# Latent attention with the keys on the partitions, in place of queries on the partitions and transposed probabilities

## What is computed

```python
def mla_attend(qn, qr, kn, kr, v):
    s = (jnp.einsum('bqhd,bkhd->bhqk', qn, kn, preferred_element_type=jnp.float32)
         + jnp.einsum('bqhr,bkr->bhqk', qr, kr, preferred_element_type=jnp.float32)) * MLA_SCALE
    p = jax.nn.softmax(s, axis=-1)
    o = jnp.einsum('bhqk,bkhd->bqhd', p.astype(v.dtype), v)
    return o.reshape(qn.shape[0], qn.shape[1], H_B * V_B)
```

## Time and profile before

| | us |
|---|---|
| median of 3 runs | 3316.15 |
| lowest and highest of the runs | 3316.11, 3319.95 |
| span of the profiled execution | 3312.2 |
| the stage, first product to the first of `mix_and_route` | 305.3 |
| TensorE busy in the span | 3117.9 (94%) |
| VectorE, ScalarE, GpSimd busy in the span | 1331.6, 780.3, 621.2 |

### The profile page before, as it was taken

The page is one execution under the profiler, slowest core; times in us unless marked ns, Lnnn a source line. Parts: engine busy times, 40 slices in busy tenths (PEclk is TensorE's granted clock), DMA queues, the critical chain, the costliest instruction groups (busy, mean ns, idle before and its releaser), DMA issues. The chain is left out here.

```text
span 3312.2 us, 35441 instructions
## 1 busy us (share of the span) xinstructions
PE 3117.9 (94%) x14154; PEld 1647.6 (50%) x14154; DVE 1331.6 (40%) x2223; ACT 780.3 (24%) x1548; POOL 621.2 (19%) x519
## 2 busy tenths in 40 slices
PE   7998989999949999599999988999999999999998
PEld 3457656665424444244456656444444444444443
DVE  2226437673351111524322465314525444544233
ACT  3126534442211111312212036111011211111001
POOL 0005400000000110023022125322203232321323
PEclk9999999999969999699999999999999999999999
DMA  7210000003267885501000130012101111113443
GB/s 287 76 51 29 1 26 1 1 1 155 115 249 295 331 332 174 202 32 38 29 24 27 52 134 2 32 51 95 70 38 51 51 39 39 50 38 141 137 132 130
DMA packets 65826, 311.38 MB, mean 94 GB/s; under 512 B 10240, under 2 KB 11776, under 8 KB 51840
## 3 DMA queue, kind: packets, MB, share of 16 engines
q1 hardware_dynamic: 61056, 292.35, 23.6%
q0 software_dynamic: 4608, 16.78, 2.0%
HBM read 272.39 MB, written 36.70 MB: 93 GB/s over the span
## 5 line engine op out<-in xcount | busy, mean ns | idle before, releaser
L2697 PE MATMUL banks<-hT,ffn_ring 128*128 128x512 f32 x528 | 235.7, 596 | 1.1 <-PEq L2393 1.1
L2857 PE MATMUL banks<-down_ring,down_sums 128*128 128x512 f32 x440 | 189.2, 592 | 0.0
L2697 PEld LDWEIGHTS banks<-hT,ffn_ring 128*128 128x128 f32 x528 | 101.0, 192 | 128.4 <-issue 128.3
L822 PE MATMUL banks<-kT_b,qT_b 96*128 96x512 f32 (+1 forms) x384 | 158.7, 523 | 3.5 <-ACT prob_b L884 2.4
L2697 PE MATMUL banks<-ffn_row_sums,ffn_w_sums 128*128 128x512 f32 x352 | 158.3, 592 | 1.2 <-DVE ffn_row_sums L2737 1.2
L330 PE MATMUL banks<-w_in,hT 128*128 128x512 f32 (+1 forms) x384 | 157.5, 567 | 1.2 <-PEq L157 1.2
L2747 DVE SCALAR_TENSOR_TENSOR ffn_acc<-ffn_u,s_ffn_taps,ffn_acc 128x1023 f32<-128x1023 f32 x88 | 125.0, 1421 | 68.0 <-ACT ffn_acc L2730 66.4
L2857 PEld LDWEIGHTS banks<-down_ring,down_sums 128*128 128x128 f32 x440 | 83.6, 190 | 105.2 <-issue 103.8
L728 POOL TENSOR_TENSOR prob<-prob,softmax_columns 128x640 f32<-128x640 f32 (+1 forms) x64 | 75.4, 1199 | 312.4 <-DVE softmax_columns L686 312.4
L1592 PE MATMUL banks<-hT,side_ring 128*128 128x512 f32 x256 | 127.5, 617 | 1.3 <-PEq L2208 1.3
L2666 POOL TENSOR_TENSOR ffn_w_sums<-ffn_ring 128x512 f32<-128x512 f32 x22 | 35.1, 1596 | 473.8 <-DMA ffn_ring<-in_w_ffn 344.2
(11 more groups left out here) (509 smaller groups left out, 5379.4 us busy)
## 6 DMA issues: line engine op xcount, KB each, us to landing
down_ring<-in_w_down SPq DMA_DIRECT2D x132, 256.0 KB, 2.9
expert_wg<-in_w_gate SPq DMA_DIRECT2D x16, 2048.0 KB, 15.4
expert_wu<-in_w_up SPq DMA_DIRECT2D x16, 2048.0 KB, 20.8
expert_wd<-in_w_down SPq DMA_DIRECT2D x16, 2048.0 KB, 8.5
ffn_ring<-in_w_ffn SPq DMA_DIRECT2D x22, 1024.0 KB, 4.8
wmod_slab<-in_w_mod SPq DMA_DIRECT2D x6, 2048.0 KB, 7.9
wmod_ring<-in_w_mod SPq DMA_DIRECT2D x4, 2048.0 KB, 10.9
w_out<-in_w_out SPq DMA_DIRECT2D x4, 2048.0 KB, 8.5
```

The costliest lines, as they stand in the source:

```text
L822: last = nc.tensor.matmul(scores(u)[:, a:b], heads[u // 2].q[u % 2], heads[u // 2].keys[u % 2][:, a:b], start=True, stop=True, skip_group_ ...
L2697: last = nc.tensor.matmul(product(f, m), wt[:, q, :], x[:, q, :], start=q == 0 and m != 2, stop=q == 3, skip_group_check=True)
L2857: last = nc.tensor.matmul(c.bank(4 - 4 * (p % 2) + t), stationary[:, P * t:P * t + P], w[s % RING][:, 0, :], start=j == 0, stop=j == N - 1)
```

## The change

`attend_by_keys` takes the place of `attend_latent`. Its unit `u` is a pair of heads and 256 queries; there are 16. The scores are made the other way round, with 128 keys on the partitions and 2 x 256 queries along the row: ten key tiles `j` of 128 x 512, one PSUM bank each, four banks in turn. Probabilities then have the keys on the partitions, as the value product wants them, and aren't transposed. What the softmax needs over the keys lies across partitions now:

- `evict`: ScalarE copies each score tile to SBUF (`prob`).
- `highest`: VectorE keeps a running maximum `top` over the tiles. It reads each tile from its bank, after ScalarE's copy of it (nine instructions of 512 columns for each unit).
- `turn`: TensorE transposes `top` (four pieces); `highest_of`: VectorE reduces it to the negated maximum of each query; `spread_max`: TensorE spreads that over the partitions (bank 5).
- `shift`: VectorE adds it to two key tiles at a time (five instructions of 1024 columns). `exponents`: ScalarE takes the exponents, also two tiles at a time.
- GpSimd adds the ten tiles up to `acc` (four additions of 1024 columns, one of 512). `total`: TensorE sums that over the partitions (four products with one column). `invert`, `spread_inverse`: VectorE inverts, TensorE spreads the inverse.
- `mix`: ten pairs of value products of 256 columns, in two runs of five tiles. `take`: VectorE copies the spread inverse and multiplies the product by it.

Beside that, the load of the first half of `w_out` waits until half of the scores are made (its place is now that of keys no longer used), and in `mix_and_route` the clearing of `aff` stands behind the first eight tiles of VectorE.

```diff
@@ in place of attend_latent @@
+            def score(u, j):
+                g = NK * u + j
+                if g >= 4:
+                    if (g - 4) % NK == 0:
+                        pe.wait_ge(evicted, g - 3)
+                    else:
+                        pe.wait_ge(maxed, highest_upto(g - 4))
+                for e in range(2):
+                    last = nc.tensor.matmul(score_bank(g)[:, QB * e:QB * e + QB], units[u].keys[e][:, P * j:P * j + P], units[u].q[e], start=True, stop=True, skip_group_check=True)
+                last.then_inc(scored, 1)
...
+            for u in range(n + 2):
+                for j in range(NK):
+                    if u < n:
+                        score(u, j)
+                    if j == 1 and 1 <= u <= n:
+                        turn(u - 1)
+                    if j == 2:
+                        if u >= 2:
+                            for i in range(NK // 2, NK):
+                                mix(u - 2, i)
+                        if 1 <= u <= n:
+                            spread_max(u - 1)
+                    if j == 6 and u >= 2:
+                        total(u - 2)
+                    if j == 7:
+                        if u >= 2:
+                            spread_inverse(u - 2)
+                        if 1 <= u <= n:
+                            for i in range(NK // 2):
+                                mix(u - 1, i)
...
+            def highest(u, j):
+                g = NK * u + j
+                dve.wait_ge(evicted, g + 1)
...
+                    dve.wait_ge(maxed, highest_upto(g - 1))
+                    nc.vector.tensor_tensor(top[:, :], score_bank(g), top[:, :], ALU.max).then_inc(maxed, 1)
+            def shift(u, i):
+                if i == 0:
+                    dve.wait_ge(spread, u + 1)
...
+                nc.vector.tensor_tensor(tiles(u, i), tiles(u, i), c.bank(5).unsqueeze(1).to_broadcast([P, 2, 2 * QB]), ALU.add).then_inc(shifted, 1)
+            def take(u):
+                dve.wait_ge(spread_back, u + 1)
+                dve.wait_ge(mixed, NK * u + NK)
+                nc.vector.tensor_copy(k.inverse[:, :], product(u)[:, QB:2 * QB]).then_inc(taken_one, 1)
+                dve.wait_ge(taken_one, u + 1)
+                nc.vector.tensor_tensor(units[u].out, product(u)[:, 0:QB], k.inverse[:, :], ALU.mult).then_inc(taken, 1)
...
+            for u in range(n + 2):
+                for j in range(NK):
+                    if j == 1 and 1 <= u <= n:
+                        highest_of(u - 1)
+                    if j and j % 2 == 0 and 1 <= u <= n:
+                        shift(u - 1, j // 2 - 1)
+                    if j == 9 and 1 <= u <= n:
+                        shift(u - 1, 4)
+                    if u < n and j:
+                        highest(u, j)
+                    if j == 6 and u >= 2:
+                        invert(u - 2)
+                    if j == 8 and u >= 2:
+                        take(u - 2)
...
+            def evict(u, j):
+                g = NK * u + j
+                act.wait_ge(scored, g + 1)
+                if u >= 2:
+                    act.wait_ge(mixed, NK * (u - 2) + j + 1)
+                    act.wait_ge(summed, 5 * (u - 2) + max(j // 2, 1))
+                nc.scalar.activation(tile(u, j), score_bank(g), ACT.Identity).then_inc(evicted, 1)
...
+            for u in range(n + 2):
+                for j in range(NK):
+                    if u < n:
+                        evict(u, j)
+                    if j == 0 and u >= 2:
+                        exponents(u - 2, 4)
+                    if j >= 3 and j % 2 and 1 <= u <= n:
+                        exponents(u - 1, j // 2 - 1)
@@ first_attention @@
     def out_weights(sp, scored):
+        sp.wait_ge(scored, NK * len(units) // 2)
         sp.dma_start(k.w_out[0][:, :, :], d["w_out"][0]).then_inc(k.w_out_in[0], 16)
@@ mix_and_route, VectorE @@
-            step(nc.vector.memset(aff[:, :, :], 0.0))
             for t in range(NT):
                 mixed(0, t)
+            step(nc.vector.memset(aff[:, :, :], 0.0))
```

More of the change, by code:

```diff
@@ L747, in _, with __init__, attend_by_keys @@
                                              ACT.Exp, bias=st[:, 1, e:e + 1], accum_out=st[:, 2, e:e + 1]).then_inc(exped, 1)
-def attend_latent(c, k, name, heads, bufs, before=None):
+class Query:
+    def __init__(self, q, keys, values, out):
+        self.q, self.keys, self.values, self.out = q, keys, values, out
+def attend_by_keys(c, k, name, units, bufs, before=None):
     nc = c.nc
[L754 to L786, removed]
@@ L788, in attend_latent, with highest_upto, tile, tiles @@
+    def highest_upto(g):
+        return (NK - 1) * (g // NK) + g % NK
+    def tile(u, j):
+        return prob[:, u % 2, j, :]
+    def tiles(u, i):
+        return prob[:, u % 2, 2 * i:2 * i + 2, :]
+    def product(u):
+        return c.bank(6 + u % 2)
     with nc.Block(no_gpsimd_drain=True) as block:
-        if before is not None:
-            block.sync(before)
+        @block.sync
+        def _(sp):
+            before(sp, scored)
         @block.tensor
         def _(pe):
[L794 to L801, removed]
-                last.then_inc(turned, 1)
[L804 to L812, removed]
-                    for e in range(2):
[L814 to L824, removed]
-            for s in range(-2, n + 2):
-                u = s + 2
-                if u < n:
-                    if u >= 2:
-                        pe.wait_ge(exped, u - 1)
-                    score(u, 0)
-                if 0 <= s < n:
-                    pe.wait_ge(evened, s + 1)
-                    turn(s, 0)
-                if u < n:
-                    if u:
-                        pe.wait_ge(exped, u)
-                    score(u, 1).then_inc(scored, 1)
-                if 0 <= s < n:
-                    turn(s, 1)
-                if s >= 2:
-                    mix(s // 2 - 1, s % 2)
-                if 0 <= s < n:
-                    turn(s, 2)
@@ new lines, in mix, with total @@
+            def mix(u, j):
+                pe.wait_ge(exped, 5 * u + j // 2 + 1)
+                if j == 0 and u >= 2:
+                    pe.wait_ge(taken, u - 1)
+                for e in range(2):
+                    last = nc.tensor.matmul(product(u)[64 * e:64 * e + 64, 0:QB], units[u].values[e][j], tile(u, j)[:, QB * e:QB * e + QB],
+                                            start=j == 0, stop=j == NK - 1, skip_group_check=True)
+                last.then_inc(mixed, 1)
+            def total(u):
+                pe.wait_ge(summed, 5 * u + 5)
+                if u == 0:
+                    pe.wait_ge(ready, 1)
+                for i in range(4):
+                    last = nc.tensor.matmul(product(u)[:, QB + i:QB + i + 1], acc[:, u % 2, 0, P * i:P * i + P], k.one[:, :],
+                                            start=True, stop=True, skip_group_check=True)
+                last.then_inc(totalled, 1)
```

120 lines of the change are left out of this document (75 added, 45 removed).

## The result

The changed kernel takes 3356.81 us (median of 4 runs, 3356.35 to 3357.31), the kernel before beside it 3316.13 (4 runs, 3312.27 to 3319.95): a ratio of 1.0122, 95% interval 1.0107 to 1.0136. It is slower by 40.7 us. I had predicted 3326.6, in a range of 3311 to 3344: the side was right, the size was not, and the time lies outside the range.

The account below looks back on a forecast made before the run. TensorE's queue bounded the old stage; the change made a VectorE-TensorE loop. Stage 314.7 against 305.33 us (+9.4), clock +1.0, on span 3312.2 gives 3322.6; plus 3.95 to the median, 3326.6, range 3311 to 3344.

Parts of the forecast that it names:

- The walk: Step-by-step count of the loop VectorE and TensorE form in each unit: 19.14 us, where it was 18.56.
- Its waits: VectorE idle 2.3 us before the first shift, 2.7 before tile 8's maximum; TensorE 1.5 before `turn`, 2 before `spread_inverse`.
- The overlap of VectorE's steps: A VectorE instruction not waiting for the one ahead starts 0.08 us before that one's end.
- the rule weighed against it: Trainium skill: VectorE's next instruction starts only once the pipe is empty; 19.8 us for each unit, 9 us more in all.
- The five waits for several semaphores: Five loop places where an instruction waits for two or three semaphores: 0 to 0.5 us for each unit, taken as 0.
- the third rival: TensorE's clock falls inside the stage, about 1.7 us each, in half to all units: 3338 to 3350; chance 0.12.
- the clock in the sum: Earlier clock drop at the stage's end, possibly a second slow stretch: 0 to 1.7 us, taken as 1.0.
- the tail: Stage end after the last maximum, with GpSimd's last additions: 20.7 us, then change of stage 1.7.
- TensorE sets the pace: Rival: VectorE's waits close, 15.7 us for each unit, 3279; needs the run of five off both ways; chance 0.10.
- GpSimd holds VectorE up: Rival: GpSimd delays VectorE's new instructions, up to 10 us for each unit; chance 0.03 together with the side-by-side pairs rival.
- The pairs lie side by side: Value products: two half-array records take 0.214 us together; rival without this +4.29 a unit, 3395, sharing 0.03 with GpSimd's.
- VectorE's steps weren't shorter: Rival: VectorE's loop steps shorter than counted, changes out cheaper; 18.1 to 18.8 us for each unit, 3312 to 3322; chance 0.19.

Follow-up runs that it names:

- e1: Changed kernel with four unused score-like products (eight records, 1.7 us) ahead of `spread_inverse` in each unit; 3335.54 us, ratio 1.0064.
- e5: Changed kernel reordered: `spread_max` right behind score tile 2, second value run behind tile 5, `spread_inverse` and first run behind tile 8; 3280.11 us.
- e6: Changed kernel with value products 0 to 4 ahead of `spread_inverse`, and maxima read from ScalarE's SBUF copy, not the bank; 3386.07 us.
- e10: e5 with the last unit's column sums made by TensorE (narrow products) instead of GpSimd; 3285.59 us, ratio 0.9909.
- e4: Changed kernel with `spread_max` ahead of the run of value products 5 to 9 instead of behind it; 3344.90 us, ratio 1.0089.
- e7: Changed kernel with `total` (eight narrow records) behind score tile 4 instead of tile 6; 3344.98 us, ratio 1.0084.
- e8b: e5 with the second value run split into single tiles, one behind each of score tiles 2 to 6; 3298.80 us, ratio 0.9948.

## Why the prediction was too low

**The walk held.** Forecast 19.14 for each unit; at full clock 19.27 (e1). Its waits were forecast as 2.3, 2.7, 1.5 and 2; in e1 they are 2.47 and 2.76 on VectorE and in the changed kernel 1.34 and 1.84 on TensorE. The overlap of VectorE's steps from the earlier trace rows is there again (605.42 starts while the maximum from 604.82 is still running), and the rule weighed against it would have given 19.8. Over 14 units (270.1 in e1) the walk was short by 2.1 us. The five waits for several semaphores, which I had taken at nothing, were not measured by themselves; the whole difference leaves 0.13 for them in each unit, unless another term was too large.

**The step that failed is the chance of the third rival,** the clock that falls inside the stage. I gave it 0.12, and counted the clock in the sum only at the stage's end, at 1.0. The text held what speaks for it: a stretch with 1.39 of 3.41 us busy was followed by a slow one, and the new waits are as long. What I did not do was to lay out the stretch around the wait at `spread_inverse`. My own walk has it: 2 us idle, one score tile (0.86), eight narrow records (0.90). Of a stretch as long as those of the earlier trace rows, that leaves 1.4 us of work, near the 1.39 that was followed by a fall and below the 1.80 that wasn't; the trace after has 1.57. The fall should have been the likeliest case. The part of the narrow records was there to be seen as well. The trace of before has a stretch in which TensorE does nothing but 30 of the 32 records of the earlier trace rows, busy for 3.27 us, and behind it the clock is at half:

```profile
26.88:30.30 3.42, 3.27 (x30) 3.18 (x29) 1.56 (x5) 3.36 (x8) 0.00 (x0) 0.99 1.09 452
30.30:33.71 3.41, 0.00 (x0) 0.00 (x0) 2.52 (x6) 2.32 (x6) 0.00 (x0) 0.50 0.94 388
```

I read their length for the sum and did not look at what came after them.

**Its size was short too.** One fall costs 1.69 as priced (1.7), and the upper end of that rival, one in each unit, is what happened: 3350. Beyond that, two units had falls of 6.83 us. The 14 full units sum to 294.9 against the forecast's 268.0: 26.9, of which 2.1 are the walk's and 24.8 the clock's. With 0.5 for the first two turns and 2.7 for the tail (25.1 from the last turn against 22.4; GpSimd's last sums and the half clock again), that is the 30.0 by which the stage is longer than forecast. The range cut this case in its middle and so had no room for it.

**Ahead of and behind the stage** the profile of after has 2.2 and 1.3 us more, where I took 1.0 for the latter and nothing for the former. Its median lies 1.3 above its span and not 3.95, which takes 2.6 back. 3326.6 + 30.0 + 2.2 + 0.3 - 2.6 = 3356.5, against 3356.8.

**The other rivals.** "TensorE sets the pace" was priced at 3279 with the condition that the run of five is off both ways; e5 does that and takes 3280.1. Its units take 15.99 where the price had 15.7, some 4 us in all, so that the last microsecond of this agreement is chance. GpSimd holds VectorE up only when both VectorE's inputs are in SBUF (e6), as written. The pairs lie side by side: a run of twenty records takes 2.38, not 4.3. VectorE's steps weren't shorter either: 19.27 at full clock, against 19.14 counted.

## What to carry to other kernels

When a change puts an engine's waits inside a stage that had none, lay out what TensorE does in the few microseconds around each new wait, narrow products and all, and compare that with the stretches of the trace that did and didn't lose the clock: the fall can cost as much as the wait that brings it on, in every turn of the loop. A row of narrow products fills TensorE's time in the trace and does not keep its clock up (e10). Idle time that looks free because another engine sets the pace is not free on TensorE. And where two engines pass work back and forth, keep long runs of work that nobody waits for out of both directions; the same products in another order took 18 to 21 us for each unit here, or 16.

## What the runs showed of the hardware

- Extra products made the kernel faster: 1.7 us of unused work in each unit brought 21 us (e1), since it kept TensorE at its 2.4 GHz level.
- A wait of 1.4 us (e4) or 1.84 us (the changed kernel, e7), once in each unit, was followed by half clock, for 3.41 us or twice that, in every full unit of e4 and of the changed kernel and in ten of 14 in e7; the wait of 1.34 at `turn`, which has score products on both sides, was not in any full unit.
- Two stretches with TensorE busy for 2.04 of 3.42 us and the same wait: the one with eight narrow records was followed by half clock, the one with score records alone was not (changed kernel, e7).
- Behind a stretch that held nothing but narrow records, 33 of them and TensorE busy for 3.40 of 3.40 us, the clock fell all the same (e10); so it did in the kernel before, behind 3.27 of 3.42 us of them.
- Going into half-array products and out again costs 0.35 us where TensorE sets the pace (e8b).
- VectorE with two SBUF inputs and GpSimd stretch each other's instructions: from 687 to 1142 ns and from 2358 to 2513 in the mean (e6).
